# Three places for the row maxima in two pipelined attentions, with a wait that looks one unit further back

## The chip, the cores and the metric

The kernel runs on one core of one Trainium2 chip. TensorE (PE in the profile, its weight loads PEld), VectorE (DVE), ScalarE (ACT), GpSimd (POOL) and the DMA queues run side by side and meet through semaphores. The metric is device time in microseconds (us) for one execution of the whole program. Lower is better.

## The reference, cut to what matters

The program is four layers over 512 tokens of width 1024, in float32. The first two mix sliding-window attention, retention and gated linear attention. The last two are an "even" and an "odd" layer, each followed by a convolutional feed-forward part. The change touches only the attentions of these last two. Cut to one form each:

```python
# even layer: differential attention (4 heads, two maps each) and three dilated banded attentions
# odd layer: compressed keys, selected blocks and a window (8 heads), and a latent attention (8 heads)
s = jnp.einsum('nbqghd,nbkgd->nbghqk', qb, kw).astype(jnp.float32) * (D ** -0.5) + bias
...
s = jnp.where((start + jnp.arange(Q_BLOCK))[:, None] >= kpos[None, :], s, -jnp.inf)
p = jax.nn.softmax(s, axis=-1).astype(v.dtype)
return jnp.einsum('bhqk,bkhd->bqhd', p, v)
```

Every softmax is: scores, scale and bias, row maximum, exponential with row sum, division by the row sum, product with the values.

## The kernel before, in words

Weights stream through a ring from HBM. Each linear stage splits them into two float32r halves and forms three products (lines 902 to 904), which is most of TensorE's time. Between linear stages stand the two attentions, `even_mix` (16 units, numbers 0 to 15) and `odd_mix` (32 units, numbers 16 to 47). A unit is a pair of heads and one block of 128 queries, with 128, 256, 384 or 512 keys, in the order 256, 512, 128, 384, which repeats every four units. In the first 16 units of `odd_mix` a unit has three groups of scores: one of 31 compressed keys (the side group, bank 4 of PSUM), and two of the full key range (banks 0 and 1, and 2 and 3). Units 32 to 47 have one group.

The engines run a software pipeline, each in program order. In step `i`

- TensorE transposes the probabilities of unit `i-3` (`turn`, line 1061), interleaved group by group with the scores of unit `i+1` (`scores`, line 1040 for the compressed keys, line 1048 for the rest), and then forms the products with the values of unit `i-4` (line 1076);
- ScalarE copies out the result of unit `i-5` (`mixed`, line 1657), takes the exponentials of unit `i-1` (`exp`, line 1641, each followed by a row that reads the accumulated row sum) interleaved with copies of the transposed blocks of unit `i-3` (`collect`, line 1650);
- VectorE scales the scores of unit `i`, adds the bias and finds the row maxima (`scaled`, line 2152, from PSUM into the buffer SE, maxima into TINY), and then normalises unit `i-2` (`normalise`, lines 2159 to 2182).

There are four SE buffers, so `scaled` of unit `u` first waits until unit `u-4` has been transposed (`at_turned`). The maxima (`UNIT_MAX`) have two places, so it also waits until all exponentials of unit `u-2`, which read their maxima as a bias, are done (`at_exp`). Only then come the waits for the scores. `normalise` of unit `u-2`, which is next in VectorE's queue, waits for the same exponentials. A score group reuses the PSUM bank of an earlier group of the previous unit, so TensorE's `scores` of unit `u+1` waits for `scaled` of unit `u`, group by group (`at_scaled`), and all that TensorE has behind it waits too.

Of the kernel before, what the change touches and what calls it, by code (L numbers as in the profile page):

```python
# [21 lines left out]
ACT = mybir.ActivationFunctionType  # L22
# [118 lines left out]
def build(nc, io, cst, out, stop=None):  # L141

    ctx = ExitStack()
    with ctx:
        ends = {"end": -(-nc.sbuf_base // 32) * 32}

        def sb(name, shape):
            ends[name], ends["end"] = ends["end"], ends["end"] + -(-4 * int(np.prod(shape)) // 32) * 32
            return nc.alloc_sbuf_tensor_at(name, [P] + shape, F32, offset=ends[name])
# [44 lines left out]
        TINY = sb("TINY", [160])  # L194
# [6 lines left out]
        IDN, STACK, ROT32, ONES_D, ONES_64, ONES_128, ONES_384, ONES_256 = (MATS[:, i, :] for i in range(8))  # L201
        EPS6, EPS5, ONE = TINY[:, 0:1], TINY[:, 1:2], TINY[:, 2:3]
        FREQ, LATE = TINY[:, 4:6], TINY[:, 6:7]
        UNIT_MAX = [TINY[:, c:c + 8] for c in (56, 152)]
        UNIT_DEN = [TINY[:, c:c + 8] for c in (64, 72, 80)]
        UNIT_RDEN = [TINY[:, c:c + 8] for c in (128, 136)]
        NMAX, DEN, RDEN = TINY[:, 152:160], TINY[:, 104:112], TINY[:, 112:120]
# [72 lines left out]
        def spare(name, offset, shape):  # L280
            return nc.alloc_sbuf_tensor_at(name, [P] + shape, F32, offset=offset)
# [9 lines left out]
        SE = [spare(f"SE{i}", ends["S"] + 4 * UNIT_AT[i], [UNIT_AT[i + 1] - UNIT_AT[i]]) for i in range(4)]  # L291
# [4 lines left out]
        def sem(name):  # L296
            return ctx.enter_context(nc.semaphore(name))
# [22 lines left out]
        at_scores, at_scaled, at_exp, at_probs, at_turned, at_turn_free, at_values, at_mixed = (  # L320
            sem(f"at_{n}") for n in ("scores", "scaled", "exp", "probs", "turned", "turn_free", "values", "mixed"))
# [373 lines left out]
        def place_left(units, pair):  # L695

            places = {4 * pair + i for i in range(4)}
            return max(n for n, u in enumerate(units) if any((u["place"] + i) % 10 in places for i in range(len(u["turns"]))))
# [751 lines left out]
        def _(act):  # L1450
            me = Side()
            fn = nc.scalar.activation
# [32 lines left out]
            def inputs(tiles, added=False, first=0, to=HI):  # L1485

                for k, t in enumerate(tiles, first):
                    if added:
                        act.wait_ge(normed, me.after(normed))
                    fn(to[:, k, :], t, ACT.Copy).then_inc(me.signals(hi_ready), 1)  # L1490
# [16 lines left out]
            def weights(upto):  # L1507

                while n_hi[0] < min(upto, len(chunks)):
                    raw, landed, _, pair, freed = chunks[n_hi[0]]  # L1510
                    act.wait_ge(*landed)
                    if freed:
                        act.wait_ge(*freed)
                    fn(WHI[pair][:, 0:raw.shape[1], :], raw, ACT.Copy).then_inc(w_hi, 1)  # L1514
                    n_hi[0] += 1
# [118 lines left out]
            def attention(units):  # L1634

                def exp(u, i):
                    act.wait_ge(at_scaled, u["maxima"][i])
                    a, c, w, at = u["softmaxes"][i]
                    c += a * u["width"]
                    x = SE[u["n"] % 4][:, c:c + w]  # L1640
                    fn(x, x, ACT.Exp, bias=UNIT_MAX[u["n"] % 2][:, at:at + 1], scale=-1.0,  # L1641
                        accum_out=UNIT_DEN[u["n"] % 3][:, at:at + 1]).then_inc(at_exp, 1)

                def collect(u, i):
                    four, at, ring = u["turns"][i], u["turn"] + i, u["ring"] + i
                    w = four[0][2]
                    act.wait_ge(at_turned, at + 1)
                    if ring >= 10:
                        act.wait_ge(at_values, OWNER[ring - 10]["done"])
                    fn(ET_SLOTS[(u["place"] + i) % 10][0:w, 0:len(four), :],  # L1650
                        PS[0:w, TURN_BANK[at], 0:len(four) * B].rearrange("p (x q) -> p x q", x=len(four)), ACT.Copy) \
                        .then_inc(at_turn_free, 1)

                def mixed(u):
                    act.wait_ge(at_values, u["done"])
                    out = PS[:, 7, 0:2 * B].rearrange("p (a q) -> p a q", a=2) if u["diff"] else PS[:, 7, 0:B]
                    fn(u["dst"], out, ACT.Copy).then_inc(me.signals(at_mixed), 1)

                def squares():
                    act.wait_ge(*me.last)  # L1660
                    for k in range(4):
                        fn(SQ4[:, k, :], H[:, k, :], ACT.Square).then_inc(me.signals(sq_ready), 1)

                def head_rstd():
                    act.wait_ge(sub_sums, 1)
                    fn(RSUB, PS[:, 0, :], ACT.Ln, bias=EPS5).then_inc(me.signals(act_step), 1)
                    act.wait_ge(*me.last)
                    fn(RSUB, RSUB, ACT.Exp, scale=-0.5).then_inc(me.signals(sub_rstd), 1)

                def high(k):  # L1670
                    act.wait_ge(*me.last)
                    inputs([H[:, k, :]], even and k < 4, k, HI_MIXED)

                n, even = len(units), units is UNITS["even_mix"]
                for i in range(n + 5):
                    if 0 <= i - 5 < n:
                        mixed(units[i - 5])
                    if even and i == 13:
                        squares()
                    exps = range(len(units[i - 1]["softmaxes"])) if 0 <= i - 1 < n else []  # L1680
                    turns = range(len(units[i - 3]["turns"])) if 0 <= i - 3 < n else []
                    for x in range(max(len(exps), len(turns))):
                        if x < len(exps):
                            exp(units[i - 1], x)
                        if x < len(turns):
                            collect(units[i - 3], x)
                    if even and i == 16:
                        head_rstd()
                    for k in HIGHS_AT[even].get(i, ()):
                        high(k)  # L1690
                    for c in range(2):
                        if i - 5 >= max(place_left(units, chunks[at_split[0] + a][3]) for a in range(c + 1)):
                            weights(at_split[0] + c + 1)
# [172 lines left out]
            for n_met, (s, l) in enumerate(stages, 1):  # L1866
# [6 lines left out]
                if s == "mod":  # L1873
# [31 lines left out]
                    for group in VECTORS[1:]:  # L1905
                        c0, n = group[0][0], sum(n for _, n, _ in group)
# [64 lines left out]
        def _(dve):  # L1971
# [163 lines left out]
            def attention(units):  # L2135

                def scaled(u):
                    if u["n"] >= 4:
                        dve.wait_ge(at_turned, every[u["n"] - 4]["turned"])
                    buf, nmax = SE[u["n"] % 4][:, 0:2 * u["width"]].rearrange("p (a t) -> p a t", a=2), UNIT_MAX[u["n"] % 2]  # L2140
                    if u["n"] >= 2:
                        dve.wait_ge(at_exp, every[u["n"] - 2]["exps"])
                    for n, g in enumerate(u["groups"]):
                        dve.wait_ge(at_scores, g["ready"])
                        for a in range(2):
                            at = u["softmaxes"][a if u["joint"] else 2 * n + a][3]
                            score = PS[:, g["bank"], a * g["n"]:(a + 1) * g["n"]] if g["side"] else PS[:, g["bank"] + a, 0:g["n"]]
                            first = HUGE
                            if u["joint"] and n:
                                dve.wait_ge(at_scaled, g["count"] - 3 + a)  # L2150
                                first = nmax[:, at:at + 1]
                            nc.vector.tensor_tensor_reduce(buf[:, a, g["c"]:g["c"] + g["n"]], score, g["bias"][:, a, :], -u["scale"],  # L2152
                                                           first, ALU.add, ALU.min, nmax[:, at:at + 1]).then_inc(at_scaled, 1)
# [36 lines left out]
                n, every, even = len(units), UNITS["even_mix"] + UNITS["odd_mix"], units is UNITS["even_mix"]  # L2190
                for i in range(n + 2):
                    if i < n:
                        scaled(units[i])
                    if i >= 2:
                        normalise(units[i - 2])
                    if even and i == 17:
                        head_scaled()
                    if i == n + 1 and not even:
                        weights(at_split[0] + 1)
                    for k in LOWS_AT[even].get(i, ()):  # L2200
                        low(k, H[:, k, :], None, HI_MIXED)
                        if even and k == 1:
                            weights(at_split[0] + 1)
# [431 lines left out]
```

## Time and profile before

| what | value |
|---|---|
| median of 3 runs | 2121.37 us (2120.21 to 2123.31) |
| the profiled execution's own time | 2128.46 us |
| its span | 2126.7 us |
| PE busy (matmuls) | 2008.8 us, 94% |
| PEld busy | 1494.4 us, 70% |
| DVE busy | 1089.1 us, 51% |
| ACT busy | 959.7 us, 45% |
| DMA | 183.14 MB, mean 86 GB/s |

`even_mix` lies between 864 and 962 us of the span, `odd_mix` between 1528 and 1681 us. A row of the timeline reads: start in us, duration in us, engine, line of the kernel, operation, output and inputs by the program's names, number of merged instructions, and in brackets the idle time of the engine just before, with what the profile takes for its end. Start plus duration is the end of the last instruction of the row.

### The profile page before, as it was taken

How to read it: one execution, taken by the hardware profiler on the slowest of the kernel's cores; microseconds unless marked ns; L12 is line 12 of the kernel's file. 1: busy time of each engine (PE TensorE's matmuls, PEld its weight loads, DVE VectorE, ACT ScalarE, POOL GpSimd, SP SyncE). 2: the span in 40 equal slices, each digit the busy share in tenths (PEclk: the TensorE clock that was granted, in tenths of full speed). 3: DMA queues.
4: the chain of work that ended last, by engine and by line, in shares of the span. 5: the costliest groups of instructions: out<-in, count | busy, mean ns of one | idle time of the engine just before them, and what ended most of it. 6: DMA issues, size and time to landing. Idle time of an engine off the chain costs nothing.

```text
span 2126.7 us, 25345 instructions
## 1 busy us (share of the span) xinstructions
PE 2008.8 (94%) x9889; PEld 1494.4 (70%) x9889; DVE 1089.1 (51%) x2023; ACT 959.7 (45%) x1758; POOL 12.7 (1%) x28
## 2 busy tenths in 40 slices
PE   8999889999889999889999999999889999999997
PEld 3876446677456888566788888787655678888885
DVE  5623864632774322656655543442465576555333
ACT  4734664644674333574422222344676544322223
POOL 1000000000000000000000000000000000000000
PEclk8999889999989999999999999999999999999999
DMA  8431432223202533003233333324400123333331
GB/s 280 128 81 50 159 99 79 60 71 90 80 20 80 149 89 92 8 1 114 70 99 99 93 97 93 104 77 100 142 2 1 41 70 99 99 93 96 99 92 47
DMA packets 301268, 183.14 MB, mean 86 GB/s; under 512 B 17550, under 2 KB 292108, under 8 KB 299948
## 3 DMA queue, kind: packets, MB, share of 16 engines
q1 hardware_dynamic: 295437, 166.05, 26.7%
q10 hardware_dynamic: 4704, 13.31, 1.7%
q0 software_dynamic: 1008, 2.15, 0.3%
q8 instruction: 79, 1.29, 0.2%
q14 instruction: 40, 0.33, 0.0%
HBM read 179.22 MB, written 2.27 MB: 85 GB/s over the span
## 4 chain that ended last, share of the span: by engine, by line
PE 82%; DVE 8%; ACT 6%; issue 2%; DMA 1%; another core or an unknown queue 0%; ACTq 0%; DVEq 0%
PE PS L902 22%; PE PS L904 22%; PE PS L903 21%; PE PS L1048 3%; PE PS L1076 2%; PE PS L1061 2%; DVE SE L2152 1%; DVE WLO L2078 1%; PE PS L1202 1%; PE PS L1120 1%; PE PS L1225 1%; PE PS L1129 1%; PE PS L1014 1%; DVE X L2045 1%; ACT WHI L1514 1%
## 5 line engine op out<-in xcount | busy, mean ns | idle before, releaser
L903 PE MATMUL PS<-LO,WHI 128*128 128x512 f32 x1690 | 659.8, 390 | 0.0
L902 PE MATMUL PS<-HI,WHI 128*128 128x512 f32 x1578 | 626.6, 397 | 25.2 <-DVE LO L2051 10.3
L904 PE MATMUL PS<-HI,WLO 128*128 128x512 f32 x1578 | 616.7, 391 | 0.0
L2078 DVE TENSOR_TENSOR WLO<-RING,WHI 128x1024 fp32r<-128x1024 f32 (+3 forms) x271 | 314.3, 1160 | 530.9 <-ACT WHI L1514 529.9
L1514 ACT ACTIVATE WHI<-RING 128x1024 fp32r<-128x1024 f32 (+3 forms) x271 | 272.6, 1007 | 468.6 <-PE PS L904 446.7
L902 PEld LDWEIGHTS PS<-HI,WHI 128*128 128x128 f32 x1578 | 297.6, 189 | 108.5 <-issue 27.0
L903 PEld LDWEIGHTS PS<-LO,WHI 128*128 128x128 f32 x1690 | 318.5, 188 | 65.3 <-issue 1.7
L904 PEld LDWEIGHTS PS<-HI,WLO 128*128 128x128 f32 x1578 | 297.3, 188 | 62.9
L902 PE MATMUL PS<-HIDDEN,WHI 128*128 128x512 f32 x352 | 137.1, 390 | 0.6 <-PE PS L904 0.6
L904 PE MATMUL PS<-HIDDEN,WLO 128*128 128x512 f32 x352 | 137.0, 389 | 0.0
L903 PE MATMUL PS<-HIDDEN,WHI 128*128 128x512 f32 x352 | 136.9, 389 | 0.0
L1621 ACT ACTIVATE S<-PS 128x512 f32<-128x512 f32 x44 | 26.3, 597 | 179.0 <-PE PS L904 179.0
L1048 PE MATMUL PS<-Z 64*128 64x256 f32 (+7 forms) x416 | 87.4, 486 | 13.2 <-DVE TINY L2152 10.7
L1641 ACT ACTIVATE SE<-SE,TINY 128x31 f32<-128x31 f32 (+7 forms) x176 | 96.6, 551 | 2.4 <-DVE TINY L2152 2.2
L1466 ACT ACTIVATE S<-X 128x512 f32<-128x512 f32 x48 | 30.2, 632 | 127.4 <-DVE X L2127 111.6
L2107 DVE TENSOR_SCALAR E<-S,VEC 128x512 f32<-128x512 f32 x44 | 24.0, 547 | 123.0 <-ACT S L1621 122.8
L1061 PE MATMUL PS<-MATS,SE 128*128 128x128 f32 (+1 forms) x420 | 70.4, 292 | 9.1 <-ACT ETW L1650 3.5
L902 PEld LDWEIGHTS PS<-HIDDEN,WHI 128*128 128x128 f32 x352 | 66.1, 188 | 15.1 <-issue 1.4
L1061 PEld LDWEIGHTS PS<-MATS,SE 128*128 128x128 f32 (+1 forms) x420 | 46.1, 145 | 42.5 <-issue 17.1
L904 PEld LDWEIGHTS PS<-HIDDEN,WLO 128*128 128x128 f32 x352 | 66.1, 188 | 13.8
L903 PEld LDWEIGHTS PS<-HIDDEN,WHI 128*128 128x128 f32 x352 | 66.1, 188 | 13.5
L2152 DVE CUSTOM_DVE_ANT_0 SE<-PS,BIAS 128x31 f32<-128x31 f32 (+4 forms) x144 | 50.9, 411 | 47.7 <-PE PS L1061 28.6
(341 smaller groups left out, 2343.1 us busy)
## 6 DMA issues: line engine op xcount, KB each, us to landing
RING<-in_ffn_w_up SPq DMA_DIRECT2D x88, 512.0 KB, 3.7
RING<-in_w_in SPq DMA_DIRECT2D x48, 512.0 KB, 3.8
RING<-in_w_mod SPq DMA_DIRECT2D x32, 512.0 KB, 4.3
RING<-in_ffn_w_down SPq DMA_DIRECT2D x32, 512.0 KB, 4.0
RING<-in_ev_w_in SPq DMA_DIRECT2D x30, 512.0 KB, 3.8
RING<-in_w_out SPq DMA_DIRECT2D x16, 512.0 KB, 4.4
RING<-in_od_w_in SPq DMA_DIRECT2D x15, 512.0 KB, 3.9
RING<-in_ffn_w_down SPq DMA_DIRECT2D x16, 384.0 KB, 3.4
```

Source lines behind the costliest of these rows:

```text
L902: mm(bank, WHI[i2][:, i, :], hi, start=(k == 0), stop=False)
L903: mm(bank, WHI[i2][:, i, :], lo, start=False, stop=False)
L904: return mm(bank, WLO[i2][:, i, :], hi, start=False, stop=last)
L1048: ins = mm(out, g["q"][a][k], g["k"][a][k], start=(k == 0), stop=(k == last))
L1061: ins = nc.tensor.transpose(PS[0:w, TURN_BANK[at], x * B:x * B + B], buf[:, c:c + w], IDN)
L1076: ins = mm(out, v, probs, start=(i < 2), stop=(i >= last))
L1466: fn(dst, src, ACT.Square).then_inc(me.signals(sq_ready), 1)
L1514: fn(WHI[pair][:, 0:raw.shape[1], :], raw, ACT.Copy).then_inc(w_hi, 1)
L1621: fn(GPAD[:, n % 2, 2:T + 2], bank, ACT.Copy).then_inc(me.signals(acc_free_act), 1)
L1641: fn(x, x, ACT.Exp, bias=UNIT_MAX[u["n"] % 2][:, at:at + 1], scale=-1.0, accum_out=UNIT_DEN[u["n"] % 3][:, at:at + 1]).then_inc(at_exp, 1)
L2078: tt(WLO[i2][:, 0:nk, :], raw, WHI[i2][:, 0:nk, :], ALU.subtract).then_inc(me.signals(w_split), 1)
L2152: nc.vector.tensor_tensor_reduce(buf[:, a, g["c"]:g["c"] + g["n"]], score, g["bias"][:, a, :], -u["scale"], first, ALU.add, ALU.min, nmax[ ...
```

## The change

The maxima get a third place, at columns 104 to 111 of TINY (free by the time of these attentions). The unit number picks the place modulo 3 in place of modulo 2, in `exp` and in `scaled`, and `scaled` waits for the exponentials of the unit three back in place of two back.

```diff
-        UNIT_MAX = [TINY[:, c:c + 8] for c in (56, 152)]
+        UNIT_MAX = [TINY[:, c:c + 8] for c in (56, 152, 104)]
...
-                    fn(x, x, ACT.Exp, bias=UNIT_MAX[u["n"] % 2][:, at:at + 1], scale=-1.0,
+                    fn(x, x, ACT.Exp, bias=UNIT_MAX[u["n"] % 3][:, at:at + 1], scale=-1.0,
                         accum_out=UNIT_DEN[u["n"] % 3][:, at:at + 1]).then_inc(at_exp, 1)
...
-                    buf, nmax = SE[u["n"] % 4][:, 0:2 * u["width"]].rearrange("p (a t) -> p a t", a=2), UNIT_MAX[u["n"] % 2]
-                    if u["n"] >= 2:
-                        dve.wait_ge(at_exp, every[u["n"] - 2]["exps"])
+                    buf, nmax = SE[u["n"] % 4][:, 0:2 * u["width"]].rearrange("p (a t) -> p a t", a=2), UNIT_MAX[u["n"] % 3]
+                    if u["n"] >= 3:
+                        dve.wait_ge(at_exp, every[u["n"] - 3]["exps"])
```

No instruction is added, removed or moved on any engine. On VectorE, at the start of unit 2 of `even_mix`, the listing of instructions with their waits shows the only one that loses its wait altogether:

```order
@@ -662,5 +662,5 @@
 L2152 ISA SE_81,TINY<-PS,BIAS 128x512
 L2152 ISA TINY 128x1
-L2152 ISA SE_82,TINY<-PS,BIAS 128x128 [waits at_scores,at_exp]
+L2152 ISA SE_82,TINY<-PS,BIAS 128x128 [waits at_scores]
 L2152 ISA TINY 128x1
 L2152 ISA SE_82,TINY<-PS,BIAS 128x128
```

From unit 3 on the wait is still there, for a smaller count of `at_exp`. Since `normalise` of unit `u-3` stands ahead of `scaled` of unit `u` in VectorE's queue and has already waited for that count, it is always met when it is reached.

## Rows read from the trace of the kernel before

**Rows 1.** Stretch, us; busy PE, PEld, DVE, ACT, POOL; PE's granted clock; DMA share; GB/s
```profile
1565.00:1615.00 50.00, 42.88 (x378) 27.81 (x374) 33.61 (x188) 37.18 (x133) 0.00 (x0) 0.96 0.01 1
```

**Rows 2.** Line 2152, whole span: what it idled for, then who waited for it
```profile
  PE PS L1061: 43.7, 15
  ACT SE L1641: 11.6, 3
...
  PE PS L1048: 10.7, 18
  PE PS L1040: 5.0, 5
```

**Rows 3.** Timeline, three engines, around the scaling of unit 29 (512 keys)
```profile
1596.83 0.93 PE L1061 MATMUL PS<-MATS,SE 128*128 128x128 f32 x7
...
1599.43 0.20 ACT L1641 ACTIVATION_READ_ACCUMULATOR SE<-SE,TINY 128x1 f32 x1
...
1599.76 0.20 DVE L2152 CUSTOM_DVE_ANT_0 SE<-PS,BIAS 128x31 f32<-128x31 f32 x1 [3.64 <-PE PS L1061]
...
1600.24 0.40 PE L1040 MATMUL PS<-Z 128*128 128x62 f32 x2 [0.76 <-DVE TINY L2152]
...
1601.37 0.49 PE L1048 MATMUL PS<-Z 64*128 64x128 f32 x4 [0.28 <-DVE TINY L2152]
...
1602.59 0.49 PE L1048 MATMUL PS<-Z 64*128 64x128 f32 x4 [0.73 <-DVE TINY L2152]
```

**Rows 4.** Timeline, PE and DVE, around the scaling of unit 23 (384 keys)
```profile
1560.68 0.38 PE L1061 MATMUL PS<-MATS,SE 128*128 128x128 f32 x2
...
1563.23 0.20 DVE L2152 CUSTOM_DVE_ANT_0 SE<-PS,BIAS 128x31 f32<-128x31 f32 x1 [5.18 <-ACT SE L1641]
...
1563.71 0.41 PE L1040 MATMUL PS<-Z 128*128 128x62 f32 x2 [1.36 <-DVE TINY L2152]
```

**Rows 5.** Timeline, PE and DVE, around the scaling of unit 31 (384 keys)
```profile
1608.50 0.66 PE L1061 MATMUL PS<-MATS,SE 128*128 128x128 f32 x4
...
1610.04 0.41 PE L1061 MATMUL PS<-MATS,SE 128*31 128x128 f32 x2
...
1611.33 0.20 DVE L2152 CUSTOM_DVE_ANT_0 SE<-PS,BIAS 128x31 f32<-128x31 f32 x1 [3.62 <-PE PS L1061]
...
1612.67 1.33 PE L1048 MATMUL PS<-Z 64*128 64x256 f32 x8 [2.22 <-DVE TINY L2152]
```

**Rows 6.** Timeline, PE, in `even_mix`, behind the scalings of units 5, 7, 9
```profile
883.41 0.49 PE L1048 MATMUL PS<-Z 64*128 64x128 f32 x4 [0.73 <-DVE TINY L2152]
...
891.09 0.70 PE L1048 MATMUL PS<-Z 64*128 64x256 f32 x4 [0.26 <-DVE TINY L2152]
892.05 0.70 PE L1048 MATMUL PS<-Z 64*128 64x256 f32 x4 [0.25 <-DVE TINY L2152]
...
894.63 0.66 PE L1061 MATMUL PS<-MATS,SE 128*128 128x128 f32 x4 [0.34 <-DVE SE L2178]
...
902.82 0.49 PE L1048 MATMUL PS<-Z 64*128 64x128 f32 x4 [0.85 <-DVE TINY L2152]
```

**Rows 7.** Waits of PE in `odd_mix`: total us, times, longest
```profile
PE PS L1061 <- DVE SE L2182: 2.5, 3, 1.5
PE PS L1061 <- ACT ETW L1650: 0.9, 3, 0.4
```

**Rows 8.** Busy time and granted clock (columns as in Rows 1) in five stretches of `odd_mix`
```profile
1553.55:1557.18 3.63, 3.63 (x38) 3.13 (x37) 3.56 (x26) 0.46 (x2) 0.00 (x0) 0.59 0.03 7
1578.24:1580.51 2.27, 2.27 (x39) 1.92 (x37) 2.27 (x13) 0.67 (x4) 0.00 (x0) 1.00 0.00 0
1587.04:1593.01 5.97, 5.97 (x46) 3.98 (x47) 4.64 (x23) 3.13 (x13) 0.00 (x0) 0.71 0.02 5
1563.71:1568.25 4.54, 4.53 (x46) 3.12 (x47) 4.47 (x23) 3.13 (x13) 0.00 (x0) 1.00 0.00 0
1614.50:1617.90 3.40, 3.40 (x27) 2.74 (x27) 2.05 (x7) 2.61 (x10) 0.00 (x0) 0.50 0.00 0
```

## The prediction

> **What bounds the kernel now.** I read the busy times first, then the waits of the changed line, then the timeline of three engines side by side. By busy time TensorE is the busiest engine in the attentions too, but not full: in two periods of `odd_mix` it works 42.88 of 50 us, and ScalarE 37.18, VectorE 33.61 [rows 1]. So a shorter wait pays only where TensorE itself stands still, and only until ScalarE's order of work takes over.
>
> TensorE's waits for line 2152 (`scaled`) come to 10.7 + 5.0 = 15.7 us in both attentions together [rows 2]. That is the most that this edge can give directly. The question is what the scalings wait for. The view of line 2152 puts 43.7 us down to TensorE's transposes (15 times) and only 11.6 to the exponentials (3 times) [rows 2]. The ends of the rows say otherwise. Unit 29's scaling needs unit 25 transposed: the last transposes end at 1596.83 + 0.93 = 1597.76. It also needs, before the change, the exponentials of unit 27: the last row sum is read by 1599.43 + 0.20 = 1599.63. The scaling starts at 1599.76, 0.13 behind the exponentials and 2.00 behind the transposes, although its label names L1061 [rows 3]. In the units that start late in both attentions I found this 0.13 again and again, whatever the label. So the wait that the change relaxes is the one that ends last.
>
> On such labels the Trainium skill, "Perfetto Trace Analysis", section "Identifying Dependency Chains", says that an instruction that waits on several engines may have its further conditions in separate instructions ahead of it. By that reading the label can name the wrong one of the three waits; the trace agrees, by the 0.13 us above.
>
> **What each late scaling costs TensorE.** Behind unit 29 TensorE has the scores of unit 30, group by group, between transposes. It stands 0.76 us before the compressed group, 0.28 and 0.73 before the other two, 1.77 in all [rows 3]. Everything behind it is held up too: the values of unit 25, the transposes of unit 27. With the wait three back, the exponentials needed are unit 26's, which VectorE has long waited for in `normalise`. The scaling starts behind the transposes: 1597.76 + 0.13 = 1597.89, 1.87 us earlier. All three gaps are at most 1.77 together and each group's scaling moves by 1.87, so all three close. Units 21, 25 and 29 show this pattern with the same gaps: 3 x 1.77 = 5.31 us.
>
> Unit 23 (384 keys) starts at 1563.23. VectorE had been idle since 1558.05, and unit 19's transposes end at 1560.68 + 0.38 = 1561.06 [rows 4]. It could start at 1561.19, 2.04 earlier. TensorE waits only once, 1.36 us, and all of it goes. Unit 27 is the same: 2 x 1.36 = 2.72 us.
>
> Unit 31 starts at 1611.33; its buffer is free at 1608.50 + 0.66 = 1609.16, so it could start at 1609.29, also 2.04 earlier. TensorE stands for 2.22 us before the scores of unit 32 and needs 0.18 of them still [rows 5]: 2.04 us.
>
> In `even_mix` the gaps are smaller: 0.73, 0.26, 0.25, 0.34 and 0.85, sum 2.43 [rows 6]. The 0.34 is a wait for `normalise`, which stands behind the late scaling in VectorE's queue. I take all five; the lower bound is nothing.
>
> The sum is 5.31 + 2.72 + 2.04 + 2.43 = 12.5 us. The other waits for line 2152 (some 3.5 of the 15.7) lie in the filling of the two pipelines, before the exponentials of two units back can be late, and stay. So do those of the latent attention (units 32 to 47), where scalings that start earlier meet a TensorE that has no gap for them.
>
> **What may be late next.** VectorE has nothing new to do. `normalise` of unit `u-2` now starts when the exponentials are done, or when the scaling, which began earlier, is over, so it is earlier too; TensorE's waits for it are 2.5 us in three, mostly at the start [rows 7]. ScalarE's copies are the likelier next wait: it is busy 37.18 of 50, so 18.6 of a period of 25, and TensorE's own work is 21.4 of 25 [rows 1]. On average ScalarE keeps up, but it alternates exponentials and copies, and TensorE has only two banks for transposed blocks. Three such waits stand there now, 0.9 us in all, the longest 0.4 [rows 7]. Six relieved steps in `odd_mix` could each bring one: between 0 and 2.4 us. I take 0.9, since a wait of the size of those seen in about half of the steps is near what the busy times leave. That makes 12.5 - 0.9 = 11.6 us.
>
> **The clock.** The same 38 or so instructions, the values of a unit of 512 keys, take 3.63 us at a granted clock of 0.59 and 2.27 at 1.00; the same 46 instructions take 5.97 us at 0.71 and 4.54 at 1.00 [rows 8]. That is 1.36 and 1.43 us lost in two stretches in which the clock fell to the lower of its levels (1.2 for 2.4 GHz). A third such stretch starts at 1614.5 [rows 8]. All three come right behind gaps that the change closes: the 1.77 behind unit 21, the 1.36 behind unit 27, the 2.22 before unit 32. Not every such gap was followed by a fall: behind the gaps of units 23 (from 1563.71) and 25 (from 1578.24) the clock stayed at 1.00 [rows 8]. With the gaps gone I expect none of the three: 1.36 + 1.43 + 1.4 (estimated from the two) = 4.2 us. The bound below is 0 (they come elsewhere), the one above 4.2 + 2 x 1.4 = 7.0, if the shift in time took away two more such falls elsewhere in the attentions.
>
> The Trainium skill, "TensorE: Matmul & The Clock Gate", section "A second HAM failure mode: psum-queue depth-cycling", says that frequent small idle times between groups of matmuls alone make the clock go back and forth and cost throughput. By that rule the three falls belong to these gaps and the sum is 15.8; by the rows of units 23 and 25 alone, where gaps brought no fall, it would be 11.6.
>
> The forecast is 11.6 + 4.2 = 15.8 us. The profiled execution took 2128.46 us for a span of 2126.7, 0.3% above the median of the runs; I take the gain over unchanged: 2121.4 - 15.8 = 2105.6 us.
>
> **The rivals.**
> - *The clock keeps its falls.* Gaps of the pipeline's start and end stay, and the falls come at other places. Gain 11.6, time 2109.8. For it: no fall behind units 23 and 25. Against it: three falls right behind closed gaps.
> - *ScalarE's copies take over.* The second and third gap of the 512-key units (3 x 1.01), and the small ones of `even_mix` (0.85), turn into waits of the transposes for L1650, and one clock stretch comes back: 12.5 - 3.0 - 0.9 - 0.9 + 1.4 = 9.1, time 2112.3. For it: 37 of 50 busy in strict order. Against it: TensorE waits for copies 0.9 us in all now.
> - *The labels are right.* Then the transposes set 15 of the starts, and of the three that the exponentials set only unit 23's stands before a gap of TensorE: 1.4 us, time 2120.0, no change. Against it: the 0.13 us.
> - *Slower: the clock falls more often.* A wait that is always met costs nothing by itself, so only something outside the order can lose. The shift in time could put other short gaps so that the clock falls behind each. A fall costs 1.4; the direct gain is eaten by nine more than now, and it takes twelve to be measurably slower (2121.4 - 11.6 + 16.8 = 2126.6). Against it: more gaps close than could open.
>
> **Chances.** Forecast 0.60, clock keeps its falls 0.18, copies take over 0.12, labels right 0.07, slower 0.03. About 0.2% (4.2 us) is what a measurement of this kernel can tell from no change. The first three are faster by more: 0.90; same 0.07; slower 0.03. The range goes from 2102 (12.5 + 7.0 gained, 2101.9) to 2113 (the copies' case and a little more).
>
> **What would show it.** In the changed kernel's trace the scalings of units 21 to 31 start some 0.13 behind the end of the transposes of four units back. TensorE's waits for line 2152 fall from 15.7 to about 3.5. The waits for L1650 stay under 2.5. The granted clock is 1.00 from about 1545 to the end of `odd_mix`. Span near 2111. It is wrong if the scalings still start 0.13 behind exponentials, or if L1650 or L2182 stand where L2152 stood.

## The result, and the profile after

| | kernel before | changed kernel |
|---|---|---|
| median | 2120.45 us (2120.09 to 2123.31, 5 runs) | 2103.52 us (2097.71 to 2105.46, 5 runs) |
| profiled execution, its span | 2128.46, 2126.7 us | 2098.76, 2096.8 us |

The ratio is 0.9903, with a 95% interval of 0.9887 to 0.9919: a gain of 1 - 0.9903 = 0.97%, 20.6 us of 2121.4. The forecast was 15.8 us. The direction and the wait that was named were right. The gain came out larger, and the ratio puts the time at 2100.8 us, below the range that was given (2102 to 2113). The interval leaves room for 17 to 24 us. The few runs of the table are less far apart, 16.9 us in their medians and 19.3 in their means, and their median of 2103.52 lies inside the range; the ratio is what this text goes by, since two repetitions on other chips (below) come out on both sides of it.

The two profiled executions differ by 29.9 us of span, more than the medians. The table by stage shows why. The stages are the linear part ahead, `even_mix`, the linear part between, `odd_mix` and the rest, first of the kernel before:

```profile
0.00:863.76 863.76, 804.70 (x3859) 569.95 (x3859) 413.55 (x667) 433.04 (x752) 12.66 (x28) 0.95 0.33 99
863.76:962.73 98.97, 83.43 (x615) 54.27 (x612) 67.00 (x234) 68.10 (x167) 0.00 (x0) 0.95 0.02 5
962.73:1528.81 566.08, 556.27 (x2466) 441.56 (x2468) 278.88 (x353) 204.61 (x285) 0.00 (x0) 1.00 0.35 102
1528.81:1681.21 152.40, 134.06 (x1102) 83.00 (x1100) 95.73 (x476) 112.64 (x378) 0.00 (x0) 0.96 0.02 5
1681.21:2126.66 445.45, 430.37 (x1852) 345.63 (x1852) 233.94 (x293) 141.32 (x178) 0.00 (x0) 0.99 0.29 87
```

The same of the changed kernel (stretch; its length, then busy PE, PEld, DVE, ACT, POOL; granted clock; DMA share; GB/s):

```profile
0.00:856.40 856.40, 796.81 (x3859) 564.81 (x3859) 413.67 (x667) 433.36 (x752) 12.68 (x28) 0.96 0.33 100
856.40:950.29 93.89, 80.94 (x615) 52.84 (x612) 66.92 (x234) 67.91 (x167) 0.00 (x0) 0.95 0.02 4
950.29:1516.90 566.61, 556.98 (x2466) 442.16 (x2468) 279.01 (x353) 204.69 (x285) 0.00 (x0) 1.00 0.36 102
1516.90:1652.11 135.21, 126.43 (x1102) 78.99 (x1100) 95.58 (x476) 111.83 (x378) 0.00 (x0) 1.00 0.02 5
1652.11:2096.79 444.68, 430.27 (x1852) 345.60 (x1852) 234.04 (x293) 141.36 (x178) 0.00 (x0) 0.99 0.29 87
```

`even_mix` is 98.97 - 93.89 = 5.08 us shorter and `odd_mix` 152.40 - 135.21 = 17.19. Another 7.36 us lie ahead of `even_mix`, in work that both kernels do alike. The granted clock is 0.95 there against 0.96, with 81.9 us in all at the lower clock against 61.4. The profiles of the runs below put that stage anywhere between 855.6 and 863.8 us, with the wait two back or three. So it is chance, and only the ratio of the runs tells the gain. A part of the 5.08 us is chance too. The last row of products in `even_mix`, 32 matmuls, reads before, after, and in a third profile of the changed kernel in which the clock is at its full level there:

```profile
958.87 3.45 PE L1076 MATMUL PS<-ETW,Z 128*64 128x128 f32 x32 [2.05 <-ACT H L1657]
```

```profile
947.27 2.62 PE L1076 MATMUL PS<-ETW,Z 128*64 128x128 f32 x32 [2.05 <-ACT H L1657]
```

```profile
955.16 1.97 PE L1076 MATMUL PS<-ETW,Z 128*64 128x128 f32 x32 [2.05 <-ACT H L1657]
```

3.45 - 2.62 = 0.83 us come from where a stretch at the lower clock fell. They leave 5.08 - 0.83 = 4.25.

In the two attentions one can split the gain further: the length less PE's busy time is its idle time. In `even_mix` that goes from 15.54 to 12.95 (2.59 less), in `odd_mix` from 18.34 to 8.78 (9.56 less). The rest is busy time: 2.49 less in `even_mix`, at the same mean clock, and 7.63 less in `odd_mix`, where the clock rose from 0.96 to 1.00.

Line 2152 in the changed kernel, which answers to [rows 2]: what it idled for, then who waited for it:

```profile
  PE PS L1061: 40.6, 18
...
  ACT SE L1641: 0.4, 1
...
  PE PS L1048: 3.4, 7
```

TensorE's waits for the scalings fell from 15.7 to 3.4 us, and the row for the compressed group (L1040) is gone. VectorE's own idle time ahead of the line hardly moved under the label L1061 (43.7 to 40.6), since VectorE has slack. Only the waits of TensorE count.

The waits of PE in `odd_mix`, which answer to [rows 7]:

```profile
PE PS L1061 <- DVE SE L2182: 2.2, 2, 1.5
PE PS L1061 <- ACT ETW L1650: 1.2, 4, 0.4
PE PS L1048 <- DVE TINY L2152: 0.9, 2, 0.7
...
PE PS L1061 <- ACT MROPE L1650: 0.3, 1, 0.3
```

And the timeline around the scaling of unit 25 (512 keys), the pattern of [rows 3]:

```profile
1553.55 1.09 PE L1061 MATMUL PS<-MATS,SE 128*128 128x128 f32 x8
...
1554.68 0.20 DVE L2152 CUSTOM_DVE_ANT_0 SE<-PS,BIAS 128x31 f32<-128x31 f32 x1 [2.39 <-PE PS L1061]
...
1556.20 0.33 PE L1040 MATMUL PS<-Z 128*128 128x62 f32 x2
...
1556.32 0.20 ACT L1641 ACTIVATION_READ_ACCUMULATOR SE<-SE,TINY 128x1 f32 x1
...
1556.91 1.09 PE L1048 MATMUL PS<-Z 64*128 64x128 f32 x8
```

The transposes of unit 21 end at 1553.55 + 1.09 = 1554.64, and the scaling starts at 1554.68. The last full-range exponentials of unit 23, which the kernel before would have waited for, are read at 1556.52, 1.84 us later. TensorE has no bracket before L1040 or L1048: all three gaps of [rows 3] are closed, and the two groups of scores, two rows there, stand here as one. (Idle times under 0.15 us have no bracket; 0.11 us is left ahead of the second group.)

Two periods of `odd_mix`, which answer to [rows 1]:

```profile
1530.00:1580.00 50.00, 49.11 (x465) 33.06 (x466) 39.95 (x224) 45.35 (x162) 0.00 (x0) 1.00 0.01 2
```

TensorE is busy 49.11 of 50 us, up from 42.88, and ScalarE 45.35. This stretch is now TensorE's, at full clock.

### The profile page after: what moved, and what is told of

Read it like the earlier page. It is cut to its first block, busy times and chain, and to the rows that moved or that the text cites. A ratio compares the mean times of both kernels' runs of the same rounds, so it can differ in the third digit from the quotient of the medians.

```text
span 2096.8 us, 25344 instructions
## 1 busy us (share of the span) xinstructions
PE 1991.4 (95%) x9889; PEld 1484.4 (71%) x9889; DVE 1089.2 (52%) x2023; ACT 959.2 (46%) x1758; POOL 12.7 (1%) x28
## 4 chain that ended last, share of the span: by engine, by line
PE 84%; DVE 8%; ACT 5%; issue 1%; DMA 1%; ACTq 0%; DVEq 0%
PE PS L902 22%; PE PS L904 22%; PE PS L903 22%; PE PS L1048 3%; PE PS L1076 2%; PE PS L1061 2%; DVE SE L2152 1%; PE PS L1202 1%; DVE WLO L2078 1%; PE PS L1014 1%; DVE X L2045 1%; PE PS L1120 1%; ACT WHI L1514 1%; PE PS L1225 1%; PE PS L1234 1%
## 5 line engine op out<-in xcount | busy, mean ns | idle before, releaser
L1048 PE MATMUL PS<-Z 64*128 64x256 f32 (+7 forms) x416 | 84.3, 475 | 6.1 <-DVE TINY L2152 3.4
L1061 PE MATMUL PS<-MATS,SE 128*128 128x128 f32 (+1 forms) x420 | 67.9, 285 | 9.0 <-ACT ETW L1650 3.8
L1061 PEld LDWEIGHTS PS<-MATS,SE 128*128 128x128 f32 (+1 forms) x420 | 44.4, 141 | 41.7 <-issue 15.9
L2152 DVE CUSTOM_DVE_ANT_0 SE<-PS,BIAS 128x31 f32<-128x31 f32 (+4 forms) x144 | 50.9, 411 | 28.3 <-PE PS L1061 21.0
```

The costliest lines, as they stand in the source:

```text
L1048: ins = mm(out, g["q"][a][k], g["k"][a][k], start=(k == 0), stop=(k == last))
L1061: ins = nc.tensor.transpose(PS[0:w, TURN_BANK[at], x * B:x * B + B], buf[:, c:c + w], IDN)
```

## The experiments

Below, theory A is the prediction's: the exponentials of two units back set the late scalings, and TensorE's stops go with that wait. A "step" is the time from the first transposes of one unit to those of the next, worked out from the starts of L1061 in the trace. Between units 18 and 45, steps not named here are alike in all kernels within 0.1 us at the same clock. The experiments that change the wait all replace it by these lines, with a condition of their own, and keep the three places:

```python
back = 2 if <condition> else 3
if u["n"] >= back:
    dve.wait_ge(at_exp, every[u["n"] - back]["exps"])
```

**The kernel before, again** (no edit):

> The kernel before, unchanged, once more, for a second profile. Theory A (the profiled execution of before was an unlucky one: about 7 us of its 29.9 us distance to the profiled execution of the changed kernel lie ahead of even_mix, in more stretches at the lower clock): ratio 1.000, span near 2118 to 2121, fewer clock falls before 864 us than in the first profile, and again falls in odd_mix behind the gaps of units 17, 21, 27 or 31. Rival B (the change speeds the early stages too): span near 2126 and the falls ahead of even_mix as in the first profile.

Median 2123.17 us in 12 runs, from 2115.41 to 2132.81, against 2124.06 for its 21 partner runs: ratio 1.0003 (0.9986 to 1.0021). One kernel spreads over 17 us. `even_mix` takes 98.89 us, `odd_mix` 155.62, with 20.5 us at the lower clock, against 13.7 in the first profile. So single times and single spans are worth little here; stage lengths, steps and ratios are.

**The changed kernel, again** (no edit):

> The changed kernel, unchanged, once more. Theory A (direct gain in the two attentions some 12 to 14 us, plus clock falls that no longer come, 3 to 6 us, with a spread from falls elsewhere): ratio 0.990 to 0.994, even_mix about 94 us and odd_mix about 136 us long in the trace, no clock fall in odd_mix. Rival B (the direct gain is 12.5 less 0.9 as predicted and the rest is luck of the clock in that execution): ratio 0.9945 and at least one fall in odd_mix.

Ratio 0.9891 (0.9870 to 0.9912), `even_mix` 93.90 us, `odd_mix` 136.6. A third time, on another chip, that of the last two kernels run (one stop put back, and the second run of the other order on ScalarE):

> The changed kernel once more, beside the next one on the same chip. Theory A (direct gain 15.4 us, and no fall of the clock between steps 18 and 45 of odd_mix, since no stop of TensorE over 0.3 us stands there): ratio 0.989 to 0.991, odd_mix 135 to 137 us, all 26 steps from unit 18 to unit 44 as in the other two profiles of this kernel within 0.02 us. Rival B (falls in odd_mix come by chance about as often with or without the stops): at least one of those steps 1.4 us longer.

Ratio 0.9915 (0.9897 to 0.9933), `even_mix` 95.04 (two stretches at the lower clock lie elsewhere at its end), `odd_mix` 136.2. The three ratios are 0.9891, 0.9903 and 0.9915, with 0.9903 in the middle.

**The wait relaxed in one attention alone.** First `even_mix` (condition `u["n"] >= 16`), then `odd_mix` (condition `u["n"] < 16`):

> Three places everywhere, but in odd_mix the scalings wait for the unit two back as before. Theory A (each gap of TensorE costs its idle time and 0.25 us more, since a matmul that follows a stop isn't overlapped with its predecessor): even_mix 3.5 to 5 us shorter than before, ratio 0.9977 to 0.9983. Rival B (a gap costs its idle time): 2.4 us shorter, ratio 0.9989. odd_mix as before, about 153 us.

> Three places everywhere, but in even_mix the scalings wait for the unit two back as before. Theory A (direct 11 to 12 us, and four stretches at the lower clock that stood behind gaps of odd_mix, 1.4 to 1.6 us each, go): odd_mix about 136 us in place of 153, ratio 0.992 to 0.993. Rival B (the clock's falls are luck and come back about as often): odd_mix 141 us, ratio 0.9945.

`even_mix` alone gives 0.9966 (0.9952 to 0.9980), `odd_mix` alone 0.9934 (0.9916 to 0.9952). The stages themselves, `even_mix` and `odd_mix` of the first kernel:

```profile
856.37:950.26 93.89, 80.93 (x616) 52.84 (x613) 66.92 (x234) 67.88 (x167) 0.00 (x0) 0.95 0.02 4
1517.06:1667.48 150.42, 132.08 (x1103) 81.62 (x1101) 95.76 (x476) 112.63 (x378) 0.00 (x0) 0.97 0.02 5
```

and of the second:

```profile
856.41:955.27 98.86, 83.36 (x616) 54.19 (x613) 67.01 (x234) 68.12 (x167) 0.00 (x0) 0.95 0.02 5
1521.41:1658.20 136.79, 128.02 (x1103) 79.52 (x1101) 95.58 (x476) 111.72 (x378) 0.00 (x0) 0.99 0.02 5
```

The first ratio shows more gain than the 0.9977 to 0.9983 expected, though its interval reaches to 0.9980. Each attention shortens where its wait is relaxed and stays where it isn't. The parts add up: 0.34% and 0.66% make 1.00%, against 1.09% for both on the same chip.

**Three places, the wait still two back** (condition `True`):

> Three places for the maxima, but every scaling still waits for the exponentials of the unit two back. Theory A (the whole gain comes from the wait): ratio 1.000 within 0.002, even_mix 98.9 us, odd_mix 152 to 156 us. Rival B (part of the gain has nothing to do with the wait, such as the 7 us ahead of even_mix that every variant's profile shows and neither profile of before does): ratio about 0.9965 and even_mix begins at 856 us, not 863.

Ratio 1.0003 (0.9989 to 1.0017), `even_mix` 98.79, `odd_mix` 149.26 us. The places alone do nothing. The gain is the wait's, so for the scalings that held TensorE up the wait for the exponentials was what ended last. Not all labels L1061 of [rows 2] were wrong, though. Of the 15, six (one in `even_mix`, and units 21, 25, 27, 29 and 31; 21.3 of the 43.7 us) start 0.13 us behind a row sum of the exponentials. The other nine, seven of them in the latent attention, start 0.04 us behind the end of the transposes, and there the label is right. So the label still stands for 40.6 us after the change. This kernel also gives the lower clock a price. Its `odd_mix` has two stretches of 3.4 us at the lower clock, the profile of before has four, the repetition 20.5 us, which is six. The lengths are 149.26, 152.40 and 155.62: about 1.55 us for each stretch, and 146.2 us without any. (The kernel with `even_mix` alone relaxed has three in `odd_mix` and takes 150.42, 0.4 less than this makes. One stretch within a single step costs 1.4 to 1.7.) The 149.26 is below the 152 to 156 expected, since this profile has only two.

**Some of the units alone.** Only the 384-key units 23, 27 and 31 three back (condition `u["n"] not in (23, 27, 31)`), then only the 512-key units (condition `u["n"] not in (21, 25, 29)`):

> Three places; only the scalings of units 23, 27 and 31 wait three back, all others two back. Theory A (a step of TensorE shortens by its gaps and by what a stop costs beyond them, and clock falls go with the gaps): the steps of these units as in the changed kernel (4.97, 4.98 and 4.6 us between first transposes of units 20-21, 24-25, 28-29), no fall after the ones behind units 23 to 31, odd_mix 144 to 148 us, ratio 0.996 to 0.998. Rival B (clock falls are spread by chance): odd_mix shorter by the direct 5 us only, with falls behind the relieved units too.

> Three places; only the scalings of units 21, 25 and 29 wait three back, all others two back. Theory A: three steps of 6.2 us become 4.23 us (5.9 us in all), the fall behind unit 21 goes, those behind 27 and before 32 can stay: odd_mix 143 to 148 us, ratio 0.996 to 0.998; with the run of the 384-key units alone it adds up to the 15 to 18 us of odd_mix alone. Rival B (the last waits only change places: relieving some moves the stall to the others): the two runs together give clearly less than odd_mix alone.

Ratios 0.9985 (0.9971 to 0.9998) and 0.9967 (0.9955 to 0.9979). The steps in us, with a star where a stretch at the lower clock lies in them:

```
step                 before   384 only  512 only  changed
18-19 (512)           7.77*     6.19      4.23      4.23
19-20                 4.77      4.77      5.34      4.77
20-21 (384)           6.30      4.97      6.30      4.97
21-22                 6.06      6.21      6.07      6.06
22-23 (512)           6.19      7.77*     4.24      4.23
23-24                 4.77      4.76      4.99      4.77
24-25 (384)           7.73*     4.98      6.30      4.98
25-26                 6.07      6.21      6.07      6.06
26-27 (512)           6.20      7.80*     4.23      4.24
27-28                 4.77      4.77      4.98      4.77
28-29 (384)           8.31*     4.61      9.56*     4.61
30-31                 4.39      4.40      4.40      4.03
```

At full clock a 512-key step loses 6.19 - 4.23 = 1.96 us and a 384-key step 6.30 - 4.97 = 1.33. Each follows from its own unit. The steps behind them give a little back as long as the other kind is late: 0.57, 0.22 and 0.21 us in the 512-only kernel, 0.15 twice in the 384-only one. That is 1.0 and 0.3 us, and the 0.37 of step 30-31 comes only with both. The halves make 0.15% + 0.33% = 0.48% where both kinds make 0.66%, 3.8 us more, where the expectation was that the halves add up; the 1.7 us of the steps are part of it, and the rest is within the intervals. The two halves themselves can't be ranked: their medians are 2118.24 and 2118.00 us, their `odd_mix` 146.03 and 145.77.

The stretches at the lower clock change places: in the 384-only kernel steps 22-23 and 26-27 have one, which had none in the first profile, while 18-19 has none. That alone doesn't show an effect of the edit, since they change places without one too. In the repetition of the kernel before they lie in steps 18 to 20, 22-23, 24-25 and 28-29, with the places alone in 24-25 and 28-29, with `even_mix` alone relaxed in 20-21 and 28-29. What all have in common is that they come with a stop that is left, though not with each. The step 22-23 of the 384-only kernel, in PE's timeline:

```profile
1566.59 0.40 PE L1040 MATMUL PS<-Z 128*128 128x62 f32 x2 [0.75 <-DVE TINY L2153]
...
1567.72 0.49 PE L1048 MATMUL PS<-Z 64*128 64x128 f32 x4 [0.28 <-DVE TINY L2153]
1568.94 0.59 PE L1048 MATMUL PS<-Z 64*128 64x128 f32 x4 [0.73 <-DVE TINY L2153]
```

and the clock right behind them:

```profile
1569.20:1572.60 3.40, 3.40 (x32) 2.85 (x32) 3.32 (x24) 0.84 (x4) 0.00 (x0) 0.50 0.00 0
```

**One stop put back** (the changed kernel with the condition `u["n"] == 25`; a single run):

> The changed kernel, but unit 25 alone waits for the exponentials of unit 23 as before. Theory A (the stops behind one scaling cost TensorE 1.96 us, and a fall of the clock, if one comes, comes right behind them): step 22-23 takes 6.19 us, or 7.8 with a fall, and every other step from 18 to 44 is as in the changed kernel; odd_mix 137.2 or 138.7 us. Rival B (ScalarE or VectorE makes the stall up within the following units, as TensorE is not the bound there): step 22-23 is 6.19, but the steps behind it are shorter than in the changed kernel.

One run, 2108.77 us. Steps 22-23 and 23-24 take 8.47 and 5.59 us, against 4.23 and 4.77; all others are those of the changed kernel. `odd_mix` takes 140.26 us, more than the 138.7 expected with a fall, since the stretch is twice as long as supposed and reaches into the next step. In PE's timeline:

```profile
1562.16 0.40 PE L1040 MATMUL PS<-Z 128*128 128x62 f32 x2 [0.75 <-DVE TINY L2153]
...
1563.30 0.49 PE L1048 MATMUL PS<-Z 64*128 64x128 f32 x4 [0.28 <-DVE TINY L2153]
1564.52 0.80 PE L1048 MATMUL PS<-Z 64*128 64x128 f32 x4 [0.73 <-DVE TINY L2153]
```

and the clock behind them, then after it has risen:

```profile
1564.52:1571.22 6.70, 6.70 (x49) 5.45 (x49) 4.97 (x32) 2.29 (x12) 0.00 (x0) 0.50 0.00 0
1571.22:1574.54 3.32, 3.32 (x23) 1.73 (x24) 0.32 (x5) 2.92 (x7) 0.00 (x0) 0.99 0.01 2
```

The one edit costs (8.47 - 4.23) + (5.59 - 4.77) = 5.06 us: 1.96 of the stop and 3.10 of a clock that stays at the lower level (1.2 for 2.4 GHz) for 6.8 us, although TensorE is busy in all of it. Nothing else differs, and this part of the changed kernel has no such stretch in any of its three profiles. One profile alone could be chance, but all thirteen agree. In the seven that have late scalings left among units 21 to 31, steps 18 to 45 hold 15 stretches, at least one in each profile, and every one starts between 0.9 us before and 2.0 us behind the end of a stop for `scaled`. In the six that have none left, those steps hold no stretch, although stops of up to 0.42 us for other causes remain.

**What stands next: ScalarE at the end of `even_mix`.** In the changed kernel PE waits there 4.3 us for L1657 (`mixed`):

```profile
PE PS L1076 <- ACT H L1657: 4.3, 2, 2.2
PE PS L1061 <- DVE SE L2178: 2.7, 2, 1.9
PE PS L1061 <- ACT ETW L1650: 2.6, 4, 1.0
PE PS L1048 <- DVE TINY L2152: 2.4, 5, 0.7
```

ScalarE has other small work queued ahead of that copy, so I put it later:

```diff
-        HIGHS_AT = {True: {18: (0, 1), 19: (2, 3, 4)},
+        HIGHS_AT = {True: {19: (0, 1, 2, 3, 4)},
...
+                    if even and i == 17:
+                        head_rstd()
...
-                    if even and i == 16:
-                        head_rstd()
```

> The changed kernel, and at the end of even_mix ScalarE copies out unit 12 before it waits for the head sums, and copies out unit 14 before the first two high halves of the next stage. Theory A (after the change what is left of TensorE's stops in even_mix is ScalarE's order: 2.20 and 2.05 us before L1076): these two gaps shrink to under 0.5 each and the time falls by 2 to 4 us more, ratio 0.988 to 0.990. Rival B (the next stage's start waits for the high halves instead): even_mix no shorter than 93.9 us, ratio as that of the changed kernel.

> The kernel with ScalarE's changed order at the end of even_mix once more. Theory A (3.1 us less in even_mix, 1.0 given back at the start of the next stage): 2 us below the changed kernel, ratio lower by 0.001. Rival B (all of it given back, or drowned in the spread of the clock's falls ahead of it): no difference that the runs can tell.

Ratios 0.9891 (0.9874 to 0.9907) and 0.9898 (0.9881 to 0.9916). `even_mix` takes 90.80 us, 3.1 less, and the following stage about 1 us more. PE's waits in `even_mix`:

```profile
PE PS L902 <- DVEq L2605: 2.8, 1, 2.8
...
PE PS L1076 <- ACT H L1657: 0.9, 1, 0.9
```

L1657 fell from 4.3 to 0.9: one of the two gaps is gone, the other is 0.87 where under 0.5 was expected. A wait of 2.8 for VectorE's queue is new. The stage is shorter by more than the difference of the waits, since its mean clock is 0.98 in place of 0.95: the two stretches at its end are gone in both profiles of this kernel. One lies in the following stage instead, at 949.84 us, and has its part in the 1 us given back. Beside the changed kernel on the same chip (0.9915) the second run of it is 0.0017 lower, 3.6 us, and the intervals overlap. A net 2 us in the stages is likely; the times don't tell it from nothing.

## Why the prediction was right or wrong

**Which wait ends last: right.** With the places alone the time is 1.0003 of before; with the wait relaxed the scaling of unit 25 starts 1.84 us ahead of the exponentials that the old wait named. The scalings of units 21, 23, 25, 27, 29 and 31 start 0.04 us behind the end of the transposes, not 0.13 as expected: these ends are modelled.

**The idle time that goes: right.** 12.5 less 0.9 made 11.6 us. The idle time of PE fell by 2.59 + 9.56 = 12.15 us. The waits for L2152 went from 15.7 to 3.4, as expected (3.5). L1650 went from 0.9 to 1.2 + 0.3 = 1.5 in `odd_mix`, an increase of 0.6 where 0.9 stood; the largest new wait is the 0.28 us of a 384-key step.

**What a closed gap is worth: the step that failed.** The prediction took each gap at its idle time, under "What each late scaling costs TensorE". With the clock's part taken out, the attentions became shorter by 4.3 us in `even_mix` and 146.2 - 135.2 = 11.0 in `odd_mix`, 15.3 in all, where the term was 11.6. PE's idle time gives 12.15 of them; the other 3.2 are in its busy time, which the prediction put at nothing, and the first gap of [rows 6] shows it. PE before, the row ahead of that gap and the row of [rows 6] behind it (883.41, four matmuls of 0.49 in all):

```profile
882.19 0.49 PE L1048 MATMUL PS<-Z 64*128 64x128 f32 x4
```

and the same eight matmuls after:

```profile
874.70 0.71 PE L1048 MATMUL PS<-Z 64*128 64x128 f32 x8
```

Before, they take from 882.19 to 883.41 + 0.49 = 883.90, 1.71 us. After, they take 0.71. One stop of 0.73 idle us cost 1.00, because the matmuls behind a stop don't overlap those ahead of it: 0.49 + 0.49 in two pieces is 0.71 in one. For the other stops only the lengths of the steps are measured. This whole step got 1.10 shorter. In `even_mix` the terms 0.73, 0.26 + 0.25 + 0.34 and 0.85, 2.43 in all, came out as 1.10, 1.56 and 1.34; with 0.15 and 0.14 in two steps where no gap was counted that is 4.29 us, alike in every profile with this wait relaxed, and the rest of the 5.08 is the clock's, by the row of products at the stage's end (0.83). In `odd_mix` the 512-key steps gave 1.96 for 1.77, and the 384-key steps 1.33 for 1.36, with a new wait of 0.28 taken off. (In the idle time of the 512-key steps 0.11 us remains.) The step of unit 31 gave about 2.2 for 2.04 (8.31 - 4.61 less one clock stretch, since no profile has that step unrelieved at full clock), and step 30-31, where nothing was counted, another 0.37 that neither half brings alone. Why that step shortens, and the two of `even_mix`, no run shows. A second, smaller error is the deduction of 0.9 for ScalarE's copies: the new waits are 0.6 and are contained in the measured steps.

**The clock: right in kind, and in size as far as it can be told.** The term was 4.2 us for three stretches. The gain of 20.6 less the direct 15.3 leaves 5.3. Stage lengths give it in another way: `odd_mix` takes 151.9 us on average in the four profiles with its wait two back throughout, and 136.4 in the six with it relaxed; 15.5 less the direct 11.0 is 4.5. In the profiles with the wait two back in all of `odd_mix` it had 2 to 6 such stretches of 3.4 us, four of them in the profile that the prediction read, which counted the three behind closed gaps. Two of these begin 0.15 and 0.18 us behind the gap's end, the third, at 1614.5, 1.85 us behind it. In the profiles with the wait relaxed there is none in steps 18 to 45, apart from the stop put back. The granted clock was 1.00 through the whole of `odd_mix` in the first profile; in others one stretch stands at the stage's start, before the relaxed units, or up to three at its very end. By the rule of the Trainium skill that the prediction cited ("TensorE: Matmul & The Clock Gate", "A second HAM failure mode: psum-queue depth-cycling"), frequent small idle times between groups of matmuls bring such changes. The traces agree in kind, by the seven profiles with such stops and the six without; in the run with the stops of one scaling put back, a single group of three was enough.

**The rivals.** "The labels are right": refuted for the scalings that held TensorE up, by the third place with and without the relaxed wait; true for the nine labels of starts that the change could not move. "ScalarE's copies take over": refuted; the 512-key steps fell by 1.96, where it left them 1.77 - 1.01 = 0.76. "The clock keeps its falls": refuted for these steps; while some stops are left, as in the 384-only kernel, falls still come with them. "Slower": nothing of it in any run.

**The sum.** 15.3 + 5.3 = 20.6 in place of 11.6 + 4.2 = 15.8. Of the 4.8 us missed, 3.7 lie in the first term: 1.9 in `even_mix`, 0.9 in `odd_mix`, and the 0.9 deducted. The clock's 5.3 is a remainder; the 0.8 between it and the 4.5 from the stage lengths is inside the interval of the ratio. The span of 2096.8, against 2111 expected, holds another 7.4 us of chance from ahead of the attentions.

## What to carry to other kernels

When an instruction waits on several semaphores, compare its start with the ends of each candidate: the one that is always the same short time ahead is the releaser, whatever the label (here 0.13 us for ScalarE's row sums, 0.04 for the modelled ends of TensorE's transposes). Do it for each start, since one label can be right for some and wrong for others. When short stops of TensorE go, count more than the idle time, from 0.1 to 0.5 us for each stop as measured here, and take the clock apart from it by comparing steps that are free of it. Where one kernel spreads by 17 us, read stage lengths and steps, and put a gain of 1% down to a change only by ratios on one chip.

## What was not expected of the hardware

A stop of TensorE cost more than the idle time that the profile shows: 0.73 us idle cost 1.00 in the matmuls around it, and 1.10 in its step. One group of three stops, 1.76 us idle, put back alone, was followed by 6.8 us at half the granted clock, twice the usual 3.4 us (the repetition of the kernel before has such a double stretch too), while TensorE was busy without a break; that made the three stops cost 5.06 us. Which of several equal stops is followed by such a stretch could not be told in advance: step 22-23 took 6.19 us in the first profile of the kernel before and 7.85 in the second.
